# A mixing block's expert rows for the context: the weighted sum of 130 of 256 rows split by columns between VectorE and GpSimd

## The reference

```python
def peer_block(hb, w_q, sub_keys, u_tab, v_tab):
    ...                                   # scores, top 16 of each of 8 heads
    g = jax.nn.softmax(top_s, axis=-1)
    u = u_tab[expert]
    act = jax.nn.gelu(jnp.einsum('nhkd,nd->nhk', u, hb).astype(jnp.float32))
    w = (g * act).astype(hb.dtype)
    return jnp.einsum('nhk,nhkd->nd', w, v_tab[expert])
```

```python
        if not last:
            h2c = modulate(rms_norm(xc, norm2_gain[i]), csh2, csc2)
            xc = xc + cg2 * peer_ffn(h2c, peer_w_q[i], peer_sub_keys[i], peer_u[i], peer_v[i])
```

## Time and profile before

| | us |
|---|---|
| median of 3 runs | 3331.02 |
| lowest, highest | 3328.05, 3335.02 |
| the profiled execution | 3337.98 |
| its span | 3336.2 |

### The profile page before, as it was taken

How to read it: one execution, slowest core, us unless ns; L and a number is a source line. 1 busy time by engine, 2 the same in 40 slices (tenths; PEclk the granted TensorE clock), 3 DMA queues, 4 the chain that set the end, 5 groups by cost and what they waited for, 6 DMA issues and landing times. The chain is left out here.

```text
span 3336.2 us, 25178 instructions
## 1 busy us (share of the span) xinstructions
PE 2514.7 (75%) x7884; PEld 1405.4 (42%) x7884; DVE 2159.8 (65%) x5153; ACT 475.7 (14%) x1396; POOL 1326.3 (40%) x1096
## 2 busy tenths in 40 slices
PE   5786883899586499952566788887767688888887
PEld 1354553584344377421443333443334433334332
DVE  1438447687786866547867777777526577677774
ACT  0110211000111100000111111111112111111111
POOL 0000316545453656535735444454300144444442
PEclk8988885899797599975788999999978889999998
DMA  6656747889794889986859999999851299999996
GB/s 259 256 189 237 272 138 254 298 321 359 275 368 158 273 322 382 353 320 241 286 164 408 418 419 419 421 422 421 347 187 51 98 419 419 419 419 421 421 421 281
DMA packets 249209, 1046.73 MB, mean 314 GB/s; under 512 B 20550, under 2 KB 53430, under 8 KB 176884
## 3 DMA queue, kind: packets, MB, share of 16 engines
q0 software_dynamic: 147456, 805.37, 61.3%
q1 hardware_dynamic: 93728, 223.28, 18.1%
q10 hardware_dynamic: 7892, 16.48, 1.3%
HBM read 1041.28 MB, written 3.77 MB: 313 GB/s over the span
## 5 line engine op out<-in xcount | busy, mean ns | idle before, releaser
L1256 POOL DMA_INDIRECT sb_beside_slots<-in_peer_uv,sb_beside_chosen x512 | 594.6, 1161 | 446.6 <-DVE sb_xc L1246 295.1
L1227 DVE SCALAR_TENSOR_TENSOR sb_beside_slots<-sb_beside_slots,sb_beside_H 128x1024 f32<-128x1024 f32 x256 | 312.8, 1224 | 223.9 <-DMA sb_beside_slots<-in_peer_uv,sb_beside_chosen 214.4
L1246 DVE SCALAR_TENSOR_TENSOR sb_xc<-sb_beside_slots,sb_beside_small,sb_xc 128x1024 f32<-128x1024 f32 x254 | 325.9, 1283 | 4.7 <-DMA sb_beside_slots<-in_peer_uv,sb_beside_chosen 2.5
L174 PE MATMUL psum<-sb_f_arena,sb_f_ring 128*128 128x256 f32 (+1 forms) x1344 | 295.9, 383 | 7.9 <-issue 7.9
L174 PEld LDWEIGHTS psum<-sb_f_arena,sb_f_ring 128*128 128x128 f32 (+1 forms) x1344 | 251.6, 188 | 52.0 <-issue 10.0
L174 PE MATMUL psum<-sb_f_ring,sb_f_arena 128*128 128x512 f32 (+2 forms) x448 | 197.6, 603 | 5.4 <-DVE sb_f_arena L1867 5.4
L1160 PE MATMUL psum<-sb_latents_ring,sb_latents_scores 128*128 128x512 f32 x304 | 146.4, 633 | 51.2 <-ACT sb_latents_scores L1118 36.1
L1160 PE MATMUL psum<-sb_last_ring,sb_last_scores 128*128 128x512 f32 x276 | 138.6, 652 | 49.1 <-ACT sb_last_scores L1118 35.6
L1160 PE MATMUL psum<-sb_beside_slots,sb_latents_scores 128*128 128x512 f32 x288 | 141.9, 639 | 36.5 <-ACT sb_latents_scores L1118 36.5
L2149 PE MATMUL psum<-sb_f_ring,sb_f_arena 128*128 128x512 f32 x384 | 165.4, 592 | 0.0
L1016 POOL DMA_INDIRECT sb_latents_ring<-in_peer_uv,sb_latents_scores x76 | 93.2, 1227 | 127.1 <-PE psum L1160 89.7
(11 more groups left out here) (541 smaller groups left out, 4768.0 us busy)
## 6 DMA issues: line engine op xcount, KB each, us to landing
sb_f_ring<-in_w_ff SPq DMA_DIRECT2D x32, 2048.0 KB
sb_context_ring<-in_ada_w SPq DMA_DIRECT2D x24, 2048.0 KB, 10.8
sb_f_ring<-in_w_in SPq DMA_DIRECT2D x8, 2048.0 KB
sb_f_ring<-in_w_in SPq DMA_DIRECT2D x6, 1904.0 KB
sb_context_ring<-in_peer_w_q SPq DMA_DIRECT2D x8, 1024.0 KB, 10.0
sb_beside_slots<-in_peer_uv,sb_beside_chosen POOLq DMA_INDIRECT x512
sb_f_ring<-in_w_out SPq DMA_DIRECT2D x4, 2048.0 KB
sb_latents_ring<-in_peer_w_q SPq DMA_DIRECT2D x8, 1024.0 KB, 18.1
```

What stands on the lines that cost most here:

```text
L174: last = e.matmul(out, a, b, start=(i == 0), stop=(i == len(terms) - 1))
L1227: e.scalar_tensor_tensor(out=self.u_slot[s % 4], in0=self.u_slot[s % 4], scalar=1.0, in1=self.H[:, s // (PH * TOPK), :], op0=ALU.mult, op1 ...
L1246: e.scalar_tensor_tensor(out=acc, in0=row, scalar=wn, in1=acc, op0=ALU.mult, op1=ALU.add).then_inc(self.added, 1)
L1256: return e.indirect_dma_start(out=to, out_offset=None, in_=self.table, in_offset=bass.IndirectOffsetOnAxis(ap=at, axis=0), element_offset= ...
```

## The change

`beside.vector` gets an argument `shared`. It is true in the middles of both layers and in the latents' attention, which makes rows 0 to 30, 103 to 133 and 188 to 255 of v shared rows: 31 + 31 + 68 = 130 of 256. For a shared row VectorE adds columns 0 to 639 (`SPLIT`), and GpSimd adds columns 640 to 1023 in two instructions: a TENSOR_SCALAR that multiplies 384 columns of the slot by the weight in place, and a TENSOR_TENSOR that adds them to `sb_xc`. In the two rows that begin a context tile one TENSOR_SCALAR does both. GpSimd does its part of row n in step n + 18, behind the u gather of that step and ahead of its v gather. A v gather now waits for both parts of the row that had its slot (`added`, `pooled`). The weights have a semaphore of their own (`weighed`), for which both engines wait. An unshared row waits on VectorE for the shared ones ahead of it. GpSimd's list is two steps longer at its end.

```diff
         def more(steps):
             if beside:
-                beside.vector(e, steps)
+                beside.vector(e, steps, shared=True)
...
         if beside:
-            beside.gpsimd(e, Beside.STEPS)
+            beside.gpsimd(e, Beside.STEPS + 2)
...
-    LAG, DEEP = 16, 4
+    LAG, DEEP, SPLIT = 16, 4, 640
...
+    def parted(self, upto):
+
+        return sum(1 for n in self.shared if n < upto)
+
+    def vector(self, e, steps, shared=False):
...
-                e.tensor_tensor(w, w1, z2, ALU.mult).then_inc(*own.up())
-                e.wait_ge(*own.now)
+                if i >= self.DEEP:
+                    if self.parted(ROWS * (i - self.DEEP + 1)):
+                        e.wait_ge(self.pooled, self.parted(ROWS * (i - self.DEEP + 1)))
+                e.tensor_tensor(w, w1, z2, ALU.mult).then_inc(self.weighed, 1)
             n = s - self.LAG
             if n >= 0:
-                acc, wn, row = self.acc[n // (PH * TOPK)], self.buf(n // ROWS)[4][:, n % ROWS:n % ROWS + 1], self.v_slot[n % 4]
+                if shared:
+                    self.shared.append(n)
+                elif self.parted(n):
+                    e.wait_ge(self.pooled, self.parted(n))
+                acc, row = (a[:, 0:self.SPLIT if shared else D] for a in self.summand(n))
+                wn = self.weight(n)
+                e.wait_ge(self.weighed, n // ROWS + 1)
                 e.wait_ge(self.v_in[n % 4], 16 * (n // 4 + 1))
...
     def gpsimd(self, e, upto):
-        for s in range(self.at_gpsimd, min(upto, self.STEPS)):
+        for s in range(self.at_gpsimd, min(upto, self.STEPS + 2)):
...
+            n = s - self.LAG - 2
+            if n in self.shared:
+                acc, row = (a[:, self.SPLIT:D] for a in self.summand(n))
+                e.wait_ge(self.weighed, n // ROWS + 1)
+                e.wait_ge(self.v_in[n % 4], 16 * (n // 4 + 1))
+                if n % (PH * TOPK) == 0:
+                    e.tensor_scalar(acc, row, self.weight(n), None, ALU.mult).then_inc(self.pooled, 1)
+                else:
+                    e.tensor_scalar(row, row, self.weight(n), None, ALU.mult).then_inc(*self.scaled.up())
+                    e.wait_ge(*self.scaled.now)
+                    if self.parted(n):
+                        e.wait_ge(self.pooled, self.parted(n))
+                    whole = [m for m in range(n) if m not in self.shared]
+                    if whole:
+                        e.wait_ge(self.added, whole[-1] + 1)
+                    e.tensor_tensor(acc, acc, row, ALU.add).then_inc(self.pooled, 1)
             n = s - self.LAG + 2
             if 0 <= n < self.rows:
                 if n >= 4:
                     e.wait_ge(self.added, n - 3)
+                    if self.parted(n - 3):
+                        e.wait_ge(self.pooled, self.parted(n - 3))
                 self.gather(e, self.v_slot[n % 4], n, 1).then_inc(self.v_in[n % 4], 16)
...
-        beside.vector(e, 1)
+        beside.vector(e, 1, shared=True)
...
-        beside.vector(e, 6)
+        beside.vector(e, 6, shared=True)
```

More of the change, by code:

```diff
@@ L1200, in __init__ @@
         self.dotted, self.added, self.z_ready, self.sig_ready, self.step_sem, self.routed = sems[8:14]
+        self.weighed, self.pooled = sems[14:16]
+        self.scaled = Tally(sems[16])
         self.own = Tally(self.step_sem)
         self.at_vector = self.at_gpsimd = 0
-        self.marks = {}
+        self.marks, self.shared = {}, []
         self.rows = self.STEPS - self.LAG
@@ L1207, in buf @@
         return [self.bufs[name][:, i % self.DEEP, :] for name in ("dots", "w1", "z1", "z2", "w")]
-    def vector(self, e, steps):
+    def parted(self, upto):
+        return sum(1 for n in self.shared if n < upto)
+    def vector(self, e, steps, shared=False):
         own = self.own
@@ L1247, in vector, with summand, weight @@
         self.at_vector = min(self.at_vector + steps, self.STEPS)
+    def summand(self, n):
+        return self.acc[n // (PH * TOPK)], self.v_slot[n % 4]
+    def weight(self, n):
+        return self.buf(n // ROWS)[4][:, n % ROWS:n % ROWS + 1]
     def mark(self, name):
@@ L1810, in vector @@
         heads_out(0)
-        beside.vector(e, 2)
+        beside.vector(e, 2, shared=True)
         scores(2)
-        beside.vector(e, 1)
+        beside.vector(e, 1, shared=True)
         e.wait_ge(rstd, 6)
@@ L2207, in build @@
     with ExitStack() as ctx:
-        beside_sems = [ctx.enter_context(nc.semaphore(f"beside{i}")) for i in range(14)]
+        beside_sems = [ctx.enter_context(nc.semaphore(f"beside{i}")) for i in range(17)]
         sems = [ctx.enter_context(nc.semaphore(f"signal{i}")) for i in range(100)]
```

2 lines of the change are left out of this document (1 added, 1 removed).

## The result

The changed kernel takes 3578.97 us (median of 4 runs, 3565.03 to 3582.19) against 3333.02 us (3328.05 to 3337.47) for the kernel before on the same chip. The ratio is 1.0729, 95% interval 1.0706 to 1.0751. The forecast was 3452, its range ended at 3565. The direction and the mechanism were right, and the loss is twice as large: +246 us where +121 was the sum. The profiled execution of the changed kernel took 3565.03 us, its span is 3563.2. So the two traces differ by 227 us where the medians differ by 246.

A forecast was written before the change was run, and what follows sets the result against it. VectorE and GpSimd feed each other with little to spare, so GpSimd's longer list sets the pace. Stretch terms +36, +40, +3, +45 and -3 sum to +121 us, giving 3452 us; range 3380 to 3565.

The forecast's parts named there:

- the rival of a faster kernel: A pair under about 0.7 us is hidden in GpSimd's idle time; 0.6 of VectorE's 52 us come off, -31 us; chance 0.11.
- The price of a row: GpSimd's cost per shared row: 1.2 us for two instructions, 0.3 gaps, 0.5 waits for VectorE, together 2.0 us.
- The dear end of 2.9 us: GpSimd's row price with a slower sum and waits of 0.4 us each: 1.8 + 0.3 + 0.8 = 2.9 us.
- the five stretches: First middle +36, second middle +40, ahead of the latents' attention heads +3, heads +45, last 16 rows -3 us.
- What idle time takes up: In middles, ahead of and among the heads, 0.8 of GpSimd's idle time absorbs added work: 20, 16, 39, 17 us.
- Ahead of the heads: Latents' attention before its heads: 21 rows at 2.0 us, less 39 us of idle time, +3 us.
- among the heads: Heads of the latents' attention: 31 rows at 2.0 us, less 17 us of idle time, +45 us.
- The last 16 rows: The tail: one gather a step, so GpSimd keeps up and half of VectorE's 6 us saving counts, -3 us.
- its ways to be wrong: GpSimd still waits 15 us or more in a middle, or stretches grow without VectorE's gather waits (held, or late by a power).
- The hold of VectorE: GpSimd's 384-column reads block VectorE too: up to +86 us on top of +121, 3538; chance 0.18 shared with the dear pair.
- The dear pair: GpSimd's pair costs 2.9 us a row, sum +218 us, 3549; chance 0.18 shared with the hold of VectorE.
- The "room is enough" rival: The rival of a faster kernel: GpSimd's idle time hides the pair in all four stretches, -31 us, 3300; chance 0.11.

The follow-up runs named there:

- the kernel without the pair: The changed kernel with GpSimd's pair left out, columns 640 to 1023 of shared rows added by nobody: 3309.24 us, ratio 0.9919 to the kernel before.
- the whole sum on VectorE: The changed kernel with VectorE adding all 1024 columns and GpSimd doing its pair of 384 columns on a spare buffer: 3578.24 us, ratio 1.073.

## Why the prediction was off by a factor of two

**What bounds the kernel: right.** The two lists feed each other with little room on either. One part of it is now measured: 52 us of VectorE's time are worth 26, a little less than the 0.6 that the rival of a faster kernel took.

**The price of a row: the step that failed.** "The nearest row by work is VectorE's [...] nothing in the trace makes GpSimd the faster of the two", and so 0.61 us for each. No row supported this as more than a bound from below, and I used it as the value. The instructions take 1.24 and 0.99 us with nothing in their way, 2.24 in place of 1.2. The gaps add 0.60 in place of 0.3, since I took them from gathers that wait for other engines; none had to wait for the instruction just ahead of it. The waits for VectorE are (1371 - 1244) + (1045 - 992) ns = 0.18 us in place of 0.5. Together 3.02 for 2.0. The dear end of 2.9 us doubled the sum of two inputs and left the product at VectorE's rate; it came near by too much for the waits and too little for the rest. With 3.02 in the same sum the five stretches give +65, +69, +24, +77 and -3, that is +232 and 3563 us, against +234 in the stretches and 3579 by the medians. That it comes so near is partly luck: the sum charges 108 of the 128 rows, 60 us too little at this price, and lets idle time take up 56 us too little as well.

The Trainium skill, "GPSIMD Engine Reference", section 3.1, has 4497 ns for a sum of 2048 columns, which is 2.2 ns a column; the runs' 2.1 agree. My estimate of 0.84 us from it was still short of the 0.99 measured, as the sum of one column alone takes 0.19 us. Its section 4.1 calls one-input instructions roughly line-rate. Here the measurement differs: the TENSOR_SCALAR takes 2.5 ns a column and is the dearer of the two.

**What idle time takes up: too little.** I let 20 + 16 + 39 + 17 = 92 us be taken up, 0.85 us for each of 108 rows. Between the ends of the stretches GpSimd's waits for VectorE were 40.9, 35.5, 47.2, 24.7 and 15.1 us before and are 2.3, 1.1, 10.2, 0.6 and 0.8 us now, so 148 us were taken up. My windows of the middles ended at 616 and 1180 and left out the 15.4 and 16.0 us of waiting for the power that closes each, and I counted none in the tail. By the medians it is 128 x 3.02 - 246 = 141 us, 1.1 us a row against the kernel before; the table's 0.9 is against the faster kernel without a pair. This error hid a part of the one in the price.

**The stretches.** Both middles are 10 to 11 us below the sum at the corrected price, for the idle time just named. Ahead of the heads it is 10 us less than the corrected sum and among the heads 6 more, as GpSimd, once late, does rows there that I had counted ahead: its gathers wait for a pair 36 times among the heads, where I had 31 rows.

```profile
POOL sb_beside_slots L1276 <- POOL sb_xc L1304: 28.0, 36, 0.8
```

**The last 16 rows: wrong in sign.** "The last 16 rows have one gather a step in place of two, so GpSimd keeps up", -3 us; measured +22.6 in the last stretch, which holds 12 of them. I never priced that step. GpSimd in the tail:

```profile
1914.52 1.02 POOL L1276 DMA_INDIRECT sb_beside_slots<-in_peer_uv,sb_beside_chosen  x1 [0.78 <-POOL sb_xc L1304]
1915.58 1.27 POOL L1297 TENSOR_SCALAR sb_beside_slots<-sb_beside_slots,sb_beside_small 128x384 f32<-128x384 f32 x1
1916.93 0.99 POOL L1304 TENSOR_TENSOR sb_xc<-sb_xc,sb_beside_slots 128x384 f32<-128x384 f32 x1
1918.70 1.02 POOL L1276 DMA_INDIRECT sb_beside_slots<-in_peer_uv,sb_beside_chosen  x1 [0.78 <-POOL sb_xc L1304]
```

The step is 1918.70 - 1914.52 = 4.18 us, of which the pair with its gaps makes 3.16. VectorE waits for gathers there 9 times, 27.6 us in all. Even with my own 2.0 us the step would have been 1.0 + 2.0 + 0.3 = 3.3 us, against the 2.1 to 2.2 us from one gather to the next that the tail of before shows:

```profile
1701.31 0.94 POOL L1256 DMA_INDIRECT sb_beside_slots<-in_peer_uv,sb_beside_chosen  x1 [1.12 <-DVE sb_xc L1246]
1703.48 0.94 POOL L1256 DMA_INDIRECT sb_beside_slots<-in_peer_uv,sb_beside_chosen  x1 [1.23 <-DVE sb_xc L1246]
1705.53 0.95 POOL L1256 DMA_INDIRECT sb_beside_slots<-in_peer_uv,sb_beside_chosen  x1 [1.10 <-DVE sb_xc L1246]
```

At the end the power of the norm stands behind late rows, as the prediction named among its ways to be wrong. VectorE waits 8.46 us for it, where it waited 0.69 us before, so this is some 8 of the 22.6 us:

```profile
1947.57 1.02 POOL L1276 DMA_INDIRECT sb_beside_slots<-in_peer_uv,sb_beside_chosen  x1 [0.79 <-POOL sb_xc L1304]
1948.61 0.60 POOL L734 TENSOR_TENSOR sb_latents_small<-sb_latents_small,sb_consts 128x1 f32<-128x1 f32 x1
...
1949.24 1.62 DVE L631 SCALAR_TENSOR_TENSOR sb_latents_H<-sb_x,sb_latents_small,sb_latents_mod 128x1024 f32<-128x1024 f32 x1 [8.46 <-POOL sb_latents_small L734]
```

and before:

```profile
1720.61 1.28 DVE L631 SCALAR_TENSOR_TENSOR sb_latents_H<-sb_x,sb_latents_small,sb_latents_mod 128x1024 f32<-128x1024 f32 x1 [0.69 <-POOL sb_latents_small L734]
```

**The rivals.** The hold of VectorE is there: it is busy for 40 us more than 2159.8 - 52 (the kernel without the pair has 2107.6). It isn't on the path, as the whole sum on VectorE shows. The dear pair was the right rival for the wrong half of its reasons, and 0.18 was too little for it, since nothing in the trace bounded the price of an instruction from above. The "room is enough" rival would have needed a pair below some 1.1 us by the estimate above, and no pair between the gathers was so cheap.

## What to carry to other kernels

Price an instruction on another engine from that engine's rows; where it has none of that size, another engine's duration is not a value. Here the two instructions took 2.0 and 1.6 times VectorE's, so a range up to about twice VectorE's would have held them. Count what such an instruction does to the one behind it: a gather that waits for the result of the instruction directly ahead of it costs 0.6 us more than one with other work between. Read that engine's idle time over the whole stretch, with the waits at its ends. And moving work from a busy engine to one that feeds it pays only while the idle time takes it up: here 1.1 us a row, while the work that was moved cost 3.0 and had saved 0.4.

## What the runs showed of the hardware

- GpSimd multiplies by a scalar of each partition at 2.5 ns a column of fp32, at a shortest of 1244 ns for 384; the same product with the weight spread as a second tensor takes 816 ns. I had expected the form with fewer inputs to be the cheaper one.
- A gather behind a GpSimd instruction starts 0.78 us after its end if it waits for that instruction's semaphore, and 0.16 us after it otherwise.
- The two engines hold each other up in both directions. In the kernel with the product of two tensors, in order of time:

```profile
566.99 1.07 POOL L1297 TENSOR_TENSOR sb_beside_slots<-sb_beside_slots,sb_beside_small 128x384 f32<-128x384 f32 x1
...
567.29 1.44 DVE L1260 SCALAR_TENSOR_TENSOR sb_xc<-sb_beside_slots,sb_beside_small,sb_xc 128x640 f32<-128x640 f32 x1
568.13 1.45 POOL L1304 TENSOR_TENSOR sb_xc<-sb_xc,sb_beside_slots 128x384 f32<-128x384 f32 x1
```

VectorE's sum, 0.88 us by itself, starts while GpSimd's product runs, takes 1.44 and ends 0.67 us behind it. GpSimd's next instruction, 0.99 us by itself, starts inside VectorE's, takes 1.45 and ends 0.85 us behind it. So of each all but 0.21 and 0.14 us was still to do when the other ended. The Trainium skill, "SBUF — State Buffer", section "Who interferes with whom", has it as a full block by whichever started first; the earlier trace rows showed one direction of it, and these rows come near to it in both. In the changed kernel the time that VectorE loses by it costs nothing, as the whole sum on VectorE shows.
